# Two transformer layers on one core: candidate sums moved to GpSimd, heads interleaved, two more three-pass tiles

## The reference

```
q = (x @ w_query) -> 8 heads x 2 halves x 128
scores = q . sub_keys                      # 8 x 2 x 128 keys
top_s, top_i = top_k(scores, 16)           # per head and half
cand_s = top_s[half 0][:, None] + top_s[half 1][None, :]   # 16 x 16 sums per head
best_s, best_pos = top_k(cand_s, 16)
idx = top_i[0][best_pos // 16] * 128 + top_i[1][best_pos % 16]
gate = softmax(best_s)
y = sum over the 8 x 16 chosen experts of gate * gelu(x . u[idx]) * v[idx]
```

## Time and profile before

| | |
|---|---|
| runs | 3041.28, 3049.27, 3039.55 us (median 3041.28) |
| profiled execution | 3041.93 us, span 3040.1 us |
| mean granted clock of TensorE | 0.99 of 2.4 GHz |
| busy | PE 97%, PEld 85%, DVE 63%, ACT 45%, POOL 5% of the span |
| chosen part, layer 0 | query tiles from 159 us, up tiles from 219, gates 290 to 352, first down tile 357 |

### The profile page before, as it was taken

The page is one execution under the profiler, slowest core; times in us unless marked ns, Lnnn a source line. Parts: engine busy times, 40 slices in busy tenths (PEclk is TensorE's granted clock), DMA queues, the critical chain, the costliest instruction groups (busy, mean ns, idle before and its releaser), DMA issues. The chain is left out here.

```text
span 3040.1 us, 53591 instructions
## 1 busy us (share of the span) xinstructions
PE 2939.3 (97%) x20778; PEld 2589.8 (85%) x20778; DVE 1918.2 (63%) x3659; ACT 1352.9 (45%) x2065; POOL 147.1 (5%) x76
## 2 busy tenths in 40 slices
PE   7999999999999999899999999999998999999898
PEld 7688889899898878888989989888876988887797
DVE  4489864787647647996468874674635466553556
ACT  4442444444444544344444544444524444552444
POOL 0052000000000004300000000010000001000000
PEclk9999999999999999999999999998999999999999
DMA  5243355544555424425554355554333555323454
GB/s 204 96 176 134 122 194 180 192 155 151 193 182 192 179 104 162 151 103 193 187 187 162 146 193 186 200 188 153 112 125 145 186 191 184 144 107 142 163 182 150
DMA packets 68021, 493.57 MB, mean 162 GB/s; under 512 B 7576, under 2 KB 7584, under 8 KB 8352
## 3 DMA queue, kind: packets, MB, share of 16 engines
q1 hardware_dynamic: 67568, 490.42, 44.6%
q0 software_dynamic: 304, 1.06, 0.1%
HBM read 490.39 MB, written 1.06 MB: 162 GB/s over the span
## 5 line engine op out<-in xcount | busy, mean ns | idle before, releaser
L788 DVE TENSOR_TENSOR ring_l<-ring,tile_h 128x1024 fp32r<-128x1024 f32 x648 | 765.0, 1222 | 669.1 <-ACT tile_h L743 664.9
L743 ACT ACTIVATE tile_h<-ring 128x1024 fp32r<-128x1024 f32 x644 | 645.2, 1051 | 530.2 <-PE ps L674 445.2
L642 PE MATMUL ps<-x_h,tile_h 128*128 128x256 f32 x2016 | 575.7, 286 | 1.4 <-issue 1.2
L643 PE MATMUL ps<-x_l,tile_h 128*128 128x256 f32 x2016 | 570.2, 283 | 0.0
L644 PE MATMUL ps<-x_h,ring_l 128*128 128x256 f32 x2016 | 570.1, 283 | 0.0
L642 PEld LDWEIGHTS ps<-x_h,tile_h 128*128 128x128 f32 x2016 | 386.5, 192 | 2.3 <-issue 2.1
L643 PEld LDWEIGHTS ps<-x_l,tile_h 128*128 128x128 f32 x2016 | 386.6, 192 | 0.2
L644 PEld LDWEIGHTS ps<-x_h,ring_l 128*128 128x128 f32 x2016 | 386.4, 192 | 0.0
L747 ACT ACTIVATE arena<-ps 128x512 f32 (+1 forms) x160 | 95.6, 597 | 436.6 <-PE ps L644 346.1
L672 PE MATMUL ps<-tile_h,w_even 128*128 128x512 f32 x640 | 249.5, 390 | 3.6 <-DVE w_even L813 3.6
L672 PE MATMUL ps<-tile_h,w_odd 128*128 128x512 f32 x640 | 249.4, 390 | 0.6 <-DVE w_odd L813 0.6
(11 more groups left out here) (326 smaller groups left out, 5580.9 us busy)
## 6 DMA issues: line engine op xcount, KB each, us to landing
ring<-stream SPq DMA_DIRECT2D x464, 1024.0 KB, 4.8
cs<-consts SPq DMA_DIRECT2D x1, 1712.5 KB, 8.5
x<-x_in SPq DMA_DIRECT2D x1, 1024.0 KB, 5.3
arena<-scratch POOLq DMA_DIRECT2D x1, 1024.0 KB, 7.9
out<-x SPq DMA_DIRECT2D x2, 512.0 KB, 2.7
tab<-table SPq DMA_DIRECT2D x1, 1.0 KB, 8.6
scratch<-arena POOLq DMA_DIRECT2D x1, 12.0 KB, 5.8
```

What stands on the lines that cost most here:

```text
L642: nc.tensor.matmul(out, uh[:, c, f], x_h[:, c, :], start=(c == 0), stop=False)
L643: nc.tensor.matmul(out, uh[:, c, f], x_l[:, c, :], start=False, stop=False)
L743: nc.scalar.activation(tile_h[:, j % 2, n], slot(k + j)[:, n], ACT.Copy).then_inc(hi_ready, 1)
L788: nc.vector.tensor_tensor(low_of(k + j)[:, n], slot(k + j)[:, n], tile_h[:, j % 2, n].bitcast(F32), ALU.subtract).then_inc(lo_ready, 1)
```

## The change

- The four short additions per head leave DVE. POOL makes them as two additions over both token halves, when `top_ready` says that the 16 best of head h are there, and counts `cand_ready`. In POOL's list the sums of head h stand behind the low parts of tile h + 1 and in front of those of tile h + 2.
- On DVE a head is cut into `key_steps` and `sum_steps`. From head 2 on, the steps of head h and of the sums of head h - 2 alternate; the sums of heads 6 and 7 alternate with one another at the end. A step no longer waits right behind its instruction (`mark`, later `until`).
- `SPLIT_UPS` is 9 and `EARLY` 9: up tiles 0 to 8 are three-pass, and tile 9 is the first of those with gate groups among its matmuls (four groups per 13 pairs).
- The transposes of token half 0 come before up tile 8, those of half 1 behind it; ACT's copies likewise. DVE splits the gates of half 0, makes the one-hots of its 16 groups, and then does half 1.
- In the decoding the TENSOR_REDUCE becomes four additions in bf16 of 8, 4, 2 and 1 columns.

```diff
-EARLY = 10
+EARLY = 9
...
     def after(self, ins):
+        self.until(self.mark(ins))
+
+    def mark(self, ins):
         self.n += 1
         ins.then_inc(self.sem, 1)
-        self.eng.wait_ge(self.sem, self.layer * self.per_layer + (self.start + self.n))
+        return self.n
+
+    def until(self, n):
+        self.eng.wait_ge(self.sem, self.layer * self.per_layer + (self.start + n))
...
-        SPLIT_UPS = 7
+        SPLIT_UPS = 9
         AHEAD = 8 - FIRST_WQ + SPLIT_UPS
...
+            def sums(h):
+                pool.wait_ge(top_ready, l * 8 + (h + 1))
+                one, two, c = top[:, :, 2 * h, :], top[:, :, 2 * h + 1, :], cand[:, h % 2, :, :]
+                nc.gpsimd.tensor_tensor(c[:, :, 0:16 * WIDE].rearrange("p t (a b) -> p t a b", a=WIDE),
+                                        one[:, :, 0:WIDE].unsqueeze(3).to_broadcast([P, TT, WIDE, 16]),
+                                        two.unsqueeze(2).to_broadcast([P, TT, WIDE, 16]), ALU.add)
+                nc.gpsimd.tensor_tensor(c[:, :, 16 * WIDE:PAIRED].rearrange("p t (a b) -> p t a b", b=NARROW),
...
+                                        ALU.add).then_inc(cand_ready, 1)
+
+            low(0)
+            for h in range(8):
+                low(h + 1)
+                sums(h)
+            for n in range(9, AHEAD):
+                low(n)
...
         def groups_ahead(at):
-            return min(GROUPS, (4 * at + 10) // 11)
+            return min(GROUPS, (4 * at + 10) // 13)
...
             for j in range(EARLY - 1):
                 early_up(j)
             pe.wait_ge(key_ev, l * 8 + 8)
-            for tt in range(TT):
-                pe.wait_ge(chosen_ready, l * TT + (tt + 1))
...
+            turn_chosen(0)
             early_up(EARLY - 1)
+            turn_chosen(1)
...
+            chosen_out(0)
             act_apply(act, 1, l, A_EXP, (EARLY - 1) // 4, (EARLY - 1) % 4, ACT.Gelu)
+            chosen_out(1)
...
+            def key_steps(h):
+                rows = [(tt, 2 * h + s) for tt in range(TT) for s in range(2)]
                 dve.wait_ge(key_ev, l * 8 + (h + 1))
...
+                last.then_inc(top_ready, 1)
+                yield
+                dve.wait_ge(top_ready, l * 8 + (h + 1))
...
+            def sum_steps(h):
+                c, c2 = cand[:, h % 2, :, :], cand2[:, h % 2, :, :]
+                dve.wait_ge(cand_ready, l * 8 + (h + 1))
...
+            for h in range(2):
+                side_by_side(key_steps(h))
+            for h in range(2, 8):
+                side_by_side(key_steps(h), sum_steps(h - 2))
+            side_by_side(sum_steps(6), sum_steps(7))
...
-                    step.after(nc.vector.tensor_reduce(chosen[:, tt, s, :], hot, AX.X, ALU.add))
+                    for w in (8, 4, 2):
+                        step.after(nc.vector.tensor_tensor(hot[:, :, 0:w], hot[:, :, 0:w], hot[:, :, w:2 * w], ALU.add))
+                    step.after(nc.vector.tensor_tensor(chosen[:, tt, s, :], hot[:, :, 0], hot[:, :, 1], ALU.add))
...
-            carry_wait()
-            base = l * (2 * GROUPS)
-            with dve.Fori(0, GROUPS // 2) as i:
-                for b in range(2):
-                    one_hot(0, base, 2 * i, 16 * i + 8 * b, b)
+                carry_wait()
+                with dve.Fori(tt * GROUPS // 4, (tt + 1) * GROUPS // 4) as i:
+                    for b in range(2):
+                        one_hot(0, base, 2 * i, 16 * i + 8 * b, b)
```

More of the change, by code:

```diff
@@ L119, in after @@
     def after(self, ins):
+        self.until(self.mark(ins))
+    def mark(self, ins):
         self.n += 1
         ins.then_inc(self.sem, 1)
-        self.eng.wait_ge(self.sem, self.layer * self.per_layer + (self.start + self.n))
+        return self.n
+    def until(self, n):
+        self.eng.wait_ge(self.sem, self.layer * self.per_layer + (self.start + n))
     def close(self):
         assert self.n == self.per_layer, f"{self.n} steps"
-DVE_A, DVE_B = 132, 117
+DVE_A, DVE_B = 128, 117
 def program(nc, stream, x_in, consts, table, scratch, out):
@@ L552, in program @@
         topb = room(TT * P).bitcast(BF16).rearrange("p (t h n) -> p t h n", t=TT, h=16)
-        cand = room(TT * PAIRED).rearrange("p (t n) -> p t n", t=TT)
-        cand2 = room(TT * PAIRED).rearrange("p (t n) -> p t n", t=TT)
+        cand = room(2 * TT * PAIRED).rearrange("p (b t n) -> p b t n", b=2, t=TT)
+        cand2 = room(2 * TT * PAIRED).rearrange("p (b t n) -> p b t n", b=2, t=TT)
         best = room(TT * P).rearrange("p (t h n) -> p t h n", t=TT, h=8)
@@ L583, in program @@
         eh_ready, el_ready = sem("eh_ready"), sem("el_ready")
+        top_ready, cand_ready = sem("top_ready"), sem("cand_ready")
         FIRST_WQ = 2
-        SPLIT_UPS = 7
+        SPLIT_UPS = 9
         AHEAD = 8 - FIRST_WQ + SPLIT_UPS
@@ L850, in pool_early_lows, with low @@
         def pool_early_lows(pool, l):
-            for n in range(AHEAD):
+            def low(n):
                 k = early_tile(n)
@@ L857, in pool_early_lows @@
                                             ALU.subtract).then_inc(el_ready, 1)
+            def sums(h):
[5 more added lines that the diff above has]
+                nc.gpsimd.tensor_tensor(c[:, :, 16 * WIDE:PAIRED].rearrange("p t (a b) -> p t a b", b=NARROW),
+                                        one[:, :, WIDE:16].unsqueeze(3).to_broadcast([P, TT, 16 - WIDE, NARROW]),
+                                        two[:, :, 0:NARROW].unsqueeze(2).to_broadcast([P, TT, 16 - WIDE, NARROW]),
+                                        ALU.add).then_inc(cand_ready, 1)
[5 more added lines that the diff above has]
+                low(n)
         GROUPS = SEQ // 8
@@ L1041, in pe_block1, with turn_chosen @@
             pe.wait_ge(wq_ev, l * 8 + 8)
-            for j in range(EARLY - 1):
-                early_up(j)
-            pe.wait_ge(key_ev, l * 8 + 8)
-            for tt in range(TT):
+            def turn_chosen(tt):
                 pe.wait_ge(chosen_ready, l * TT + (tt + 1))
@@ L1049, in pe_block1 @@
                 last.then_inc(sel_mm, 1)
+            for j in range(EARLY - 1):
+                early_up(j)
+            pe.wait_ge(key_ev, l * 8 + 8)
+            turn_chosen(0)
             early_up(EARLY - 1)
+            turn_chosen(1)
             def gate_rows(base, n, b):
@@ L1202, in act_block1, with chosen_out @@
                         nc.scalar.activation(gexp[:, tt, :, :], gexp[:, tt, :, :], ACT.Exp).then_inc(g_exp, 1)
-            for tt in range(TT):
+            def chosen_out(tt):
                 act.wait_ge(sel_mm, l * TT + (tt + 1))
@@ L1312, in dve_block1 @@
             dve_split_x(dve, 2 * l + 1)
-            for h in range(8):
+            def key_steps(h):
+                rows = [(tt, 2 * h + s) for tt in range(TT) for s in range(2)]
                 dve.wait_ge(key_ev, l * 8 + (h + 1))
-                rows = [(tt, 2 * h + s) for tt in range(TT) for s in range(2)]
                 carry_wait()
@@ L1320, in dve_block1 @@
                     last = nc.vector.max(top[:, tt, r, 0:8], sc[:, tt, r, :])
-                step.after(last)
+                done = step.mark(last)
+                yield
+                step.until(done)
                 carry_wait()
@@ L1344, in dve_block1 @@
-                step.after(last)
+                    last = nc.vector.max_index(topi[:, tt, r, 8:16], top[:, tt, r, 8:16], sc2[:, n, :])
+                yield
+            def sum_steps(h):
+                c, c2 = cand[:, h % 2, :, :], cand2[:, h % 2, :, :]
+                dve.wait_ge(cand_ready, l * 8 + (h + 1))
                 carry_wait()
                 for tt in range(TT):
-                    last = nc.vector.max(best[:, tt, h, 0:8], cand[:, tt, :])
-                step.after(last)
+                    last = nc.vector.max(best[:, tt, h, 0:8], c[:, tt, :])
+                done = step.mark(last)
+                yield
+                step.until(done)
@@ L1349, in dve_block1 @@
                 carry_wait()
                 for tt in range(TT):
-                    nc.vector.max_index(pos[:, tt, h, 0:8], best[:, tt, h, 0:8], cand[:, tt, :])
-                    last = nc.vector.match_replace(cand2[:, tt, :], best[:, tt, h, 0:8], cand[:, tt, :], NEG * 1e8)
-                step.after(last)
+                    nc.vector.max_index(pos[:, tt, h, 0:8], best[:, tt, h, 0:8], c[:, tt, :])
+                    last = nc.vector.match_replace(c2[:, tt, :], best[:, tt, h, 0:8], c[:, tt, :], NEG * 1e8)
@@ L1354, in dve_block1 @@
+                done = step.mark(last)
+                yield
+                step.until(done)
                 carry_wait()
                 for tt in range(TT):
-                    last = nc.vector.max(best[:, tt, h, 8:16], cand2[:, tt, :])
-                step.after(last)
+                    last = nc.vector.max(best[:, tt, h, 8:16], c2[:, tt, :])
+                done = step.mark(last)
+                yield
+                step.until(done)
                 carry_wait()
```

(9 more changed lines are left out.)

## The result

After takes 3059.8 us (median of 10 runs, 3058.7 to 3071.8), before 3050.6 (10 runs beside them): ratio 1.0041, 95% interval [1.0029, 1.0052]: 0.4% slower. Profile against profile it is 3058.74 against 3041.93, 16.8 us more; forecast were 16.6.

What follows compares the result with a forecast made beforehand. PE, busy 97% of the span, was taken as the bound; late decoding beside POOL's subtractions costs 8.5 - 0.7 + 0.5 = 8.3 us per layer, 16.6 on 3041.9, 3058.5, so median 3058; range given 3024 to 3068 (forecast's own 3049 to 3070).

Steps and rivals of the forecast that it cites:

- Heads: DVE, interleaved heads without sums: 7.15 us a head, all sums done at about 240.6 against 254.01, 13 us earlier.
- the 8.33: DVE in before: time of a head taken to meet no POOL work (200.17 to 208.50), base for the 7.15.
- POOL's sums: Two POOL additions per head: 1.1 us, bounds 0.7 and 4.8; they wait for DVE and delay later subtractions.
- rival 3: Sums cost POOL 4.8 us a head and POOL sets the pace: 28 us later per layer, 3098; chance 0.06.
- Half 0 chosen: DVE decode of half 0: 12.75 us counted after POOL's end at 263.8, so chosen at 276.5.
- The 0.7: Decode correction per layer: DVE gains if casts and one-input operations escape POOL's block; up to 1.7 us, 0.7 taken.
- The tree: Decode's bf16 additions replacing each reduction: 1.78 us for 2.29, some 2.7 if at the f32 rate.
- First gates: PE's first gate group after half 0's gate split, loop start and one set of one-hots: at 291.5.
- The gate stretch: PE, first gate group to first down tile: 74.06 us, plus 0.5 for a 1.2 GHz clock, bounds 0 to 1.6.
- Sum: Down tiles 8.5 us late per layer, less 0.7, plus 0.5: 8.3 per layer, 16.6 in all.
- rival 2: POOL not late, ends at about 262: 1.8 to 3.4 us late per layer, 3045 to 3048; 0.20 including in-between cases.
- Rows 9 and 10: Profile rows of a POOL copy and a DVE subtraction (3.60 us, 2.15 after the copy's end), cited for blocking both ways.

Runs made afterwards that it cites:

- e1: After, with the low parts of early up tiles from the tenth on as zeros written by ScalarE instead of POOL subtractions; ratio to before 0.9941.
- e7: After, with POOL's last six subtractions held until DVE has made the halves, to lie beside all-bf16 decode steps; one run, 3058.1 us.
- e6: Before plus one part of the change alone: candidate sums on POOL and interleaved heads; ratio to before 1.0008.
- e3: After, with seven three-pass up tiles for nine and ten up tiles ahead of the gates for nine; ratio to before 0.9962.
- e2: After, with seven three-pass up tiles for nine, still nine tiles ahead of the gates; ratio to before 0.9988.
- e8: After, with before's heads (DVE sums, one after another) and ScalarE's exponentials moved behind the last early tile's high half; ratio to before 1.0050.
- e5: After, with before's heads: DVE makes the candidate sums and heads run one after another; ratio to before 1.0064.
- e9: After, with ten up tiles ahead of the gates for nine, still nine three-pass tiles; ratio to before 1.0017.

## Why the prediction was right

The mechanism is shown: the decode meets POOL's subtractions, each of its steps waits one out, and the freed DVE time is given back. Layer 0 of after starts 2.5 us earlier than before's, so 2.5 is added to after's times here.

- **Heads**: 7.0 us for 7.15 forecast, sums done at 239.7 for 240.6. Right, though the 8.33 behind it was read wrongly: head 3 does meet POOL's work (subtractions of before at 198.78 to 203.56 and 205.43 to 210.49); its four additions, 0.20 to 0.22 us each, only began just ahead of the second pair.
- **POOL's sums**: 0.75 us a head for 1.1; they wait for DVE from head 3 on, 1.6 to 1.8 us each. Right; rival 3 is gone.
- **POOL's end**: 263.4 for 263.8. Right.
- **Half 0 chosen**: 274.0 for 276.5, the first mis-sized term. I let all 12.75 us of decoding follow POOL's end; in the trace 10.6 do (260.90 to 271.49), because DVE gets one short step done per subtraction, without slowing POOL (ten in 23.86, as before's 23.88). The 0.7 that I took for casts and one-operand steps has the right sign for another reason: they don't escape, they wait like the others.
- **The tree**: 2.04 us with its gaps for 1.78, so half 1 takes 12.3 for 11.7. Half 1 is chosen at 286.3 for 288.2.
- **First gates**: 289.9 for 291.5. PE's waits (7.66, 4.30, 2.69) are those forecast.
- **The gate stretch**: 76.37 for 74.06 + 0.5, the second mis-sized term. That 74.05 holds when the clock stays at 1.00, e1 shows (103.9 to 177.9); in after it is at 0.50 until 292, which costs 2.3, beyond my bound of 1.6.
- **Sum**: +9.25 in layer 0, the two errors against each other, and +10.5 in layer 1, since before's own layer 1 is 1.2 us shorter than its layer 0. The forecast was 8.3 each, 16.6; the stages make 19.8, and level against level the runs show 19. An earlier start of 2.5 and 0.9 less between the layers, with 0.4 more behind them, make the 16.8 of the profiles. No edit explains the start: over the twelve traces it lies between 166.6 and 169.6. That 16.8 falls on 16.6 is luck, and so is 3059.8 beside 3058, since the three runs that the forecast started from had their median on before's lower level.
- **Range and rows**: 6.5 us a layer, named for the lower end, give 3054; the text does not price the part of rival 2 that would lead from there to 3049. Rows 9 and 10 show DVE waiting for POOL alone, not "both directions"; that POOL waits too e7 shows.

What the prediction did not see is how the parts share this. In layer 0, walking from before to after: sums and heads alone -2.4 (e6); turning by halves with a tile between, one-hots by halves and the tree another -4.7 (e3); the ninth tile for the tenth ahead of the gates +5.3 (e2); nine three-pass tiles for seven +11.0 (after). In layer 1 the four steps are -0.2, -5.7, +5.5 and +11.0. The forecast priced nine tiles as 2.3 us won on PE and only counted their 9.6 us on POOL inside one sum; that is where the loss is made. Rival 2 had the right lever (POOL not late) and the lesser handle: two tiles less bring POOL's end 10 to 12 us forward (e3, e2), while a POOL without sums and waits for heads ends 3.5 to 4.9 earlier (e8).

Left open: what a POOL that used its waits of 1.6 us per head for half a subtraction would bring was not tried.

## What to carry to other kernels

Before GpSimd is given more work to free TensorE, look at what VectorE does in that stretch: where that is decode arithmetic as here, each long GpSimd instruction holds up a VectorE step (MAX8 and its like were not held up, 0.29 us beside GpSimd). The price is then VectorE's delay, here some 4 us a tile (8.7 for two) where TensorE saved 1.15. When VectorE's work is moved earlier, look whether it lands beside GpSimd's; and a bundle of changes should be priced edit by edit, since here two parts won 6 to 7 us a layer and two others lost 16.

## What the hardware showed beyond that

- Short DVE steps (0.2 to 0.5 us alone) do not slow POOL while they wait for it (ten subtractions in 23.86 us in after, 2.39 each, as without them). A pair that starts while such a step is under way loses up to 0.3 (4.95 in after's last pair, 4.77 otherwise), and steps of 1.22 us cost more: 2.84 per subtraction in e7.
- The two levels come from block B. The rest of the program behind layer 1's first down tile took 1685.9 us in before, 1686.3 in after, 1696.0 in e3 and 1701.2 in e5. In e3, the first two rows below, two stretches of 100 us have a clock near 0.9; before has it in the first alone (0.91 in 2054 to 2154, 1.00 at the other's place), after in the second alone. Columns: length, busy time of PE, PEld, DVE, ACT, POOL, granted clock, DMA share, GB/s.

```profile
2040.50:2140.50 100.00, 96.90 (x712) 86.52 (x712) 51.61 (x139) 49.82 (x103) 0.00 (x0) 0.91 0.38 140
...
2540.50:2640.50 100.00, 97.00 (x708) 89.44 (x707) 49.28 (x119) 48.91 (x89) 0.00 (x0) 0.90 0.40 148
```

- Each of block B's two layers has the same work at that place: PE stands 0.6 to 0.7 us and then makes 64 short matmuls back to back. Before does it twice, in 11.87 us and in 7.33. In the first the clock falls to 0.50 2.2 us after the start, in the second it stays at 1.00:

```profile
2084.62 11.87 PE L1633 MATMUL ps<-arena,ring 128*128 128x60 f32 x64 [0.70 <-ACT arena L1797]
...
2598.85 7.33 PE L1633 MATMUL ps<-arena,ring 128*128 128x60 f32 x64 [0.61 <-ACT arena L1797]
```

- In the twelve traces the clock falls within this group 19 times of 24, 0.1 to 2.9 us after its start, and is at 0.50 for 17 to 24 us then. The five traces with one fall (before, after, e1, e7, e9) have 1685.4 to 1686.5 us behind the layers, the seven with two 1695.2 to 1701.2. The work there is the same in all twelve, so a difference of 10 us in a total does not by itself tell what an edit in block A does; what decides whether the clock falls is open.
